# Chunk loop of a delta-rule recurrence: the inverse's levels in four array quarters and in transposed form

## The chip, the cores and the metric

The kernel runs on one core of one Trainium2 chip. The metric is the device time of one execution in microseconds, the median over several; less is better. The core has a matrix engine (TensorE, PE in the profile), three elementwise engines (VectorE is DVE, ScalarE is ACT, GpSimd is POOL) and SyncE (SP), which here only issues DMAs. PE reads SBUF and writes PSUM; DVE and ACT move PSUM to SBUF; POOL works on SBUF alone.

## The reference, cut to what matters

One layer: an input projection, a gated MLP branch, an RWKV-7 branch, their merge, and a mixture of 32 experts. The change is in the RWKV-7 branch over 512 prompt tokens, 16 heads of 64:

```python
def step(s, inp):
    r_t, w_t, k_t, v_t, a_t, b_t = inp
    sa = jnp.einsum('bhij,bhj->bhi', s, a_t)
    s = s * w_t[:, :, None, :] + sa[..., :, None] * b_t[..., None, :] + v_t[..., :, None] * k_t[..., None, :]
    y = jnp.einsum('bhij,bhj->bhi', s, r_t)
    return s, y
```

The kernel doesn't step token by token. It takes 8 chunks of 64 tokens. Within a chunk the tokens depend on each other through a strictly triangular 64x64 matrix per head; with ones on the diagonal it is N, and the chunk needs the inverse of N applied to a right-hand side. The state is then carried to the next chunk.

## The kernel before, in words

`phase_chunks` is one phase between two all-engine barriers. The projections, decays and normalised keys of all tokens lie in SBUF when it starts; the next phase (`phase_gating`) begins after it.

**Tiling.** 16 heads are 8 pairs, and the two heads of a pair lie on partitions 0-63 (`lo`) and 64-127 (`hi`). The pairs are in two groups g of four (`G`, `GP`). A 64x64 block product of a head uses one quarter of the 128x128 array: its input partitions choose the quarter's rows, its output partitions the quarter's columns. Each group has four PSUM banks, `bank[g][0..3]`; bank[0][0] and bank[0][1] are halves of `m.psv`, and the profile calls them psv and the others ck_b. One float32 product is two records of the trace on PE and two on PEld. A block of eight products (one group, both heads of four pairs) is 16 records.

**The inverse.** It is built in doubling blocks: X starts as N's inverse for blocks of 2 (mask `m.levels[:, 0]`), and five levels (`LEVELS`, blocks of 2, 4, 8, 16, 32 being joined, NL = 5) make it that of 64. Z is the transposed of X, a1 the transposed of N. A level, in `level(c, lv)`:

1. PE, for g 0 then 1: W = N X by `own_blocks` (L602), weights a1, moving X, into bank 1. Eight products each.
2. DVE, per group: W into SBUF, multiplied by the level's mask (L874).
3. PE, per group: X = Z^T W (weights Z, moving W, bank 2), and but for the last level Z = W^T Z (weights W, moving Z, bank 3). Sixteen products each.
4. ACT, per group: X (L804), then Z (L807) into SBUF.

`own_blocks` reads and writes the same partitions of a head, so it uses two of the four quarters: lo to lo, hi to hi. `scores` is a block that uses all four (L639 own, L641 crossed), with 128 columns moved; `turn_bk_v` moves v to the other half (L668).

**A chunk.** PE's order is: `turn_n` (L650) for both groups, which turns N into bank 0; `turn_bk_v` for both; level 0; level 1; `old_state` (L697 to L702); levels 2, 3, 4; `scores` of the next chunk for g 0; `corrected`, which applies X to the right-hand side; `scores` for g 1; `new_state` (L715 to L722).

Around it, each engine's order is written out by hand, one queue each, with semaphores:

- DVE: the first Z is a1 times a mask (L867, two); then W per level; after W of level 2 both row products of the next chunk on the lower half (L615, L616 in `a_r_rows`); after the levels the masked scores (L828, L834), copies of the corrected values (L838), the new state (L844, L846), y (L851).
- ACT: a1 out of bank 0 (L789, two); the state (L794); per group the turned b and k (L798) and v (L799, L800); X and Z of the levels; after level 0 the exponentials of the next chunk (L770, L772); after level 1 the right-hand side (L813, L814).
- POOL: the scaled b and k of the next chunk (L623, L624), its own half of the row products, then for each group N with its diagonal (`nb`, L901) and the first X (L906).

`scores(c + 1, 0)` waits for all four row products and all four b, k products.

Of the kernel before, what the change touches and what calls it, by code (L numbers as in the profile page):

```python
# [12 lines left out]
P = 128  # L13
D = 1024
NK = D // P
TP = 512
# [100 lines left out]
def constants(eng, m, step, s_ident, wide, wide1t):  # L117
# [8 lines left out]
    step.did(eng.memset(wide1t[:, :], 0.0))  # L126
# [19 lines left out]
    for n, b in enumerate((1,) + LEVELS):  # L146
        odd = wide[:, n, :].rearrange("p (a two b) -> p a two b", two=2, b=b)[:, :, 1, :]
        step.wait()
        step.did(eng.memset(odd, 1.0))
        select(odd, ALU.is_ge, 0, [[-2 * b, P // (2 * b)], [0, b]], 1, 0.0)  # L150
        select(odd, ALU.is_ge, b - 1, [[2 * b, P // (2 * b)], [0, b]], -1, 0.0)
        select(wide[:, n, :], ALU.not_equal, 0, [[-1, P]], 1, 1.0)
    even = wide1t[:, :].rearrange("p (a two) -> p a two", two=2)[:, :, 0]
    select(even, ALU.not_equal, -1, [[-2, P // 2]], 1, 1.0)
    select(wide1t[:, :], ALU.not_equal, 0, [[-1, P]], 1, 1.0)
    step.wait()
    for half in range(2):
        own = slice(HD * half, HD * (half + 1))
        step.did(eng.tensor_copy(m.levels[own, :, :], wide[own, :, own]))
        step.did(eng.tensor_copy(m.level1t[own, :], wide1t[own, own]))  # L160
        step.did(eng.tensor_copy(m.ident2[own, :], m.ident[own, own]))
# [3 lines left out]
def phase_tokens(nc, m, a):  # L165

    ctx, sb, ps, sem = open_phase(nc)
    with ctx:
# [8 lines left out]
        wide1t = sb("wide_level1t", [P, P])  # L177
# [10 lines left out]
        @block.gpsimd  # L188
        def _(eng):
            constants(eng, m, Steps(eng, s_const), s_ident, wide, wide1t)  # L190
# [358 lines left out]
def phase_chunks(nc, m, a):  # L549

    ctx, sb, ps, sem = open_phase(nc)
    with ctx:
# [7 lines left out]
        a1 = sb("ck_a1", [P, NP, CH])  # L560
        X = sb("ck_X", [P, NP, CH])
        Z = sb("ck_Z", [P, NP, CH])
        W = sb("ck_W", [P, NP, CH])
# [10 lines left out]
        def pair_sems(name):  # L574
            return [sem(f"k_{name}{g}") for g in range(G)]

        s_eo, s_tb, s_nt, s_w, s_xz, s_rhs, s_u, s_y, s_s = \
            (pair_sems(n) for n in ("eo", "tb", "nt", "w", "xz", "rhs", "u", "y", "s"))
        s_mb, s_lk, s_nb, s_tb_e, s_a1, s_x1, s_z1, s_w_e, s_xz_e, s_rh_e, s_u_e, s_y_e, s_st, s_s0 = \
            (pair_sems(n) for n in ("mb", "lk", "nb", "tb_e", "a1", "x1", "z1", "w_e", "xz_e", "rh_e", "u_e", "y_e",  # L580
                                    "st", "s0"))
        NL = len(LEVELS)
        NX = 2 * NL - 1
# [13 lines left out]
        def own_blocks(eng, out, weights, moving, g):  # L597

            for n in range(GP):
                p = g * GP + n  # L600
                for rows in (lo, hi):
                    last = eng.matmul(out[rows, n, :], weights[rows, p, :], moving[rows, p, :], start=True, stop=True)  # L602
            return last
# [8 lines left out]
        def a_r_rows(eng, c, rows, which):  # L612

            at = tokens(c)
            eng.tensor_tensor(L[rows, :, which, 0:CH], m.kk[rows, :, at], running(c, 0, CH)[rows], ALU.mult).then_inc(s_ar, 1)  # L615
            eng.tensor_tensor(L[rows, :, which, CH:P], m.r[rows, :, at], running(c, 1, CH + 1)[rows], ALU.mult)\  # L616
# [10 lines left out]
        def _(eng):  # L627
# [17 lines left out]
            def turn_n(c, g):  # L645
                eng.wait_ge(s_nb[g], c + 1)
                eng.wait_ge(s_mb[g], c + 1)
                for n in range(GP):
                    for rows in (lo, hi):
                        last = eng.matmul(b64(bank[g][0])[rows, n, :], nb[rows, g * GP + n, :], m.ident[rows, rows],  # L650
                                          start=True, stop=True)
                last.then_inc(s_nt[g], 1)

            def turn_bk_v(c, g):
# [10 lines left out]
                for n in range(GP):  # L665
                    p = g * GP + n
                    for rows, others in ((lo, hi), (hi, lo)):
                        last = eng.matmul(b64(b[3])[others, n, :], m.v[rows, p, tokens(c)], m.ident[rows, rows],  # L668
                                          start=True, stop=True)
                last.then_inc(s_tb[g], 1)  # L670

            def level(c, lv):
                for g in range(G):
                    if lv == 0:
                        eng.wait_ge(s_a1[g], c + 1)
                        eng.wait_ge(s_x1[g], c + 1)
                        eng.wait_ge(s_lk[g], 2 * c + 2)
                    else:
                        eng.wait_ge(s_xz_e[g], c * NX + 2 * lv - 1)
                    own_blocks(eng, b64(bank[g][1]), a1, X, g).then_inc(s_w[g], 1)  # L680
                for g in range(G):
                    if lv == 0:
                        eng.wait_ge(s_z1[g], c + 1)
                        eng.wait_ge(s_tb_e[g], c * 3 + 3)
                    else:
                        eng.wait_ge(s_xz_e[g], c * NX + 2 * lv)
                    eng.wait_ge(s_w_e[g], c * NL + lv + 1)
                    own_blocks(eng, b64(bank[g][2]), Z, W, g).then_inc(s_xz[g], 1)
                    if lv < NL - 1:
                        own_blocks(eng, b64(bank[g][3]), W, Z, g).then_inc(s_xz[g], 1)  # L690

            def old_state(c, g):
                b = bank[g]
                eng.wait_ge(s_s0[g], c * 2 + 2)
                for n in range(GP):
                    p = g * GP + n
                    eng.matmul(b64(b[0])[lo, n, :], L[:, p, 0, 0:CH], wv[:, p, 0, :], start=True, stop=True)  # L697
                    eng.matmul(b64(b[0])[hi, n, :], L[:, p, 1, 0:CH], wv[:, p, 1, :], start=True, stop=True)
# [6 lines left out]
            def corrected(c, g):  # L705
                eng.wait_ge(s_rh_e[g], c * 2 + 2)
                eng.wait_ge(s_xz_e[g], c * NX + NX)
                own_blocks(eng, b64(bank[g][2]), X, rh, g).then_inc(s_u[g], 1)
# [1634 lines left out]
```

## Time and profile before

| | us |
|---|---|
| median of 3 runs | 1246.95 (1246.49 to 1248.7) |
| profiled execution, its own time | 1246.74 |
| its span | 1244.7 |
| PE busy in the span | 1123.8 (90%) |
| chunk phase, about | 279 to 490 of the span |
| mean granted clock of PE | 0.961 of full speed |

In the profile a row of a timeline is the start in the span, its duration, the engine, the line, the operation, output<-inputs, the shapes and the number of merged instructions. What stands in brackets is how long the engine stood idle before it and what released it. The end of a matmul is modelled, so starts are compared here, and a merged row's duration reaches to the modelled end of its last record. PEclk is the granted clock as a share of 2.4 GHz.

### The profile page before, as it was taken

The numbers are of one execution on the slowest core, as the hardware profiler recorded it, in microseconds if no ns is written. First come the engines' busy times: TensorE is split into PE (matmuls) and PEld (weight loads), VectorE is DVE, ScalarE is ACT, GpSimd is POOL, SyncE is SP. The second block draws the span as 40 slices with busy tenths as digits, with TensorE's granted clock in tenths as the row PEclk, the third lists the DMA queues.
The fourth block names the chain that finished last, engine by engine and source line by source line (L and its number), as shares of the span: only waits on it lengthen the run. The fifth ranks groups of instructions, "written<-read, shape, count | busy, mean of one in ns | idle before, by whom it ended". The sixth has DMA issues, their size and how long they took to land. (4 is left out here: it accounts for less than half of the span.)

```text
span 1244.7 us, 25175 instructions
## 1 busy us (share of the span) xinstructions
PE 1123.8 (90%) x10677; PEld 872.2 (70%) x10677; DVE 488.4 (39%) x1145; ACT 297.5 (24%) x584; POOL 196.7 (16%) x215
## 2 busy tenths in 40 slices
PE   3599999969999999899989999999898799988874
PEld 3488888848888988788877788888455455544441
DVE  3135455455555563455536611100236422211126
ACT  2022223334555544100024501000011111111112
POOL 4000000014354340000000007500000222211110
PEclk9799999989999999999999999999997799998897
DMA  3322122120000000322921222360776799999985
GB/s 107 95 76 59 53 53 79 26 61 14 4 4 4 4 4 3 97 66 67 236 75 34 68 68 68 87 184 1 293 318 260 268 414 415 414 417 417 415 346 206
DMA packets 113838, 182.98 MB, mean 147 GB/s; under 512 B 10364, under 2 KB 88520, under 8 KB 105029
## 3 DMA queue, kind: packets, MB, share of 16 engines
q1 hardware_dynamic: 107190, 168.56, 38.7%
q0 software_dynamic: 5168, 8.56, 1.9%
q10 hardware_dynamic: 1383, 4.42, 0.9%
q8 instruction: 79, 1.29, 0.4%
q14 instruction: 18, 0.15, 0.0%
HBM read 173.24 MB, written 17.55 MB: 153 GB/s over the span
## 5 line engine op out<-in xcount | busy, mean ns | idle before, releaser
L271 PE MATMUL rk_ps<-xT,rk_w 128*128 128x260 f32 x768 | 175.5, 387 | 9.9 <-DMA rk_lw<-in_a_lora_up 9.9
L271 PEld LDWEIGHTS rk_ps<-xT,rk_w 128*128 128x128 f32 x768 | 145.6, 191 | 37.2 <-issue 9.9
L271 PE MATMUL mg_psg<-xT,w_merge 128*128 128x260 f32 x512 | 116.6, 387 | 2.7 <-PEq L110 2.7
L271 PEld LDWEIGHTS mg_psg<-xT,w_merge 128*128 128x128 f32 x512 | 98.3, 192 | 18.1 <-issue 2.7
L2083 DVE SCALAR_TENSOR_TENSOR ex_sg<-tl_psA,ex_slot_rs,ex_sg 128x128 f32<-128x128 f32 x32 | 11.2, 351 | 139.1 <-ACT ex_sg L1883 138.9
L271 PE MATMUL uv_psu<-xT,w_uv 128*128 128x260 f32 x256 | 59.2, 391 | 3.0 <-ACTq L1037 3.0
L602 PE MATMUL ck_b<-ck_W,ck_Z 64*64 64x64 f32 x1280 | 52.3, 220 | 9.0 <-DVE ck_W L874 6.3
L271 PE MATMUL mg_psp<-ya,w_merge 128*128 128x260 f32 x256 | 57.6, 383 | 0.0
L271 PE MATMUL psv<-xT,w_uv 128*128 128x260 f32 x256 | 57.5, 383 | 0.0
L271 PE MATMUL mg_psp<-r_all,w_merge 128*128 128x260 f32 x256 | 57.4, 382 | 0.0
L271 PEld LDWEIGHTS uv_psu<-xT,w_uv 128*128 128x128 f32 x256 | 49.1, 194 | 11.0 <-ACTq L1037 3.3
L602 PEld LDWEIGHTS ck_b<-ck_W,ck_Z 64*64 64x64 f32 x1280 | 45.3, 134 | 13.3 <-issue 13.3
L1355 POOL TENSOR_TENSOR S<-S,sv 128x4096 f32<-128x4096 f32 x1 | 8.9, 8866 | 285.7 <-DVE r_all L1324 285.7
L271 PEld LDWEIGHTS mg_psp<-r_all,w_merge 128*128 128x128 f32 x256 | 48.6, 190 | 7.5
L271 PEld LDWEIGHTS psv<-xT,w_uv 128*128 128x128 f32 x256 | 48.5, 190 | 7.4
L271 PEld LDWEIGHTS mg_psp<-ya,w_merge 128*128 128x128 f32 x256 | 48.5, 190 | 7.4
L1575 POOL DMA_INDIRECT d_y<-tl_xn,ex_sidx x32 | 31.9, 998 | 118.8 <-DVE tl_xn L2087 118.8
L259 DVE TENSOR_TENSOR rk_diff<-rk_cols 128x512 f32<-128x512 f32 x24 | 16.6, 692 | 86.5 <-ACT rk_cols L451 86.5
L874 DVE TENSOR_TENSOR ck_W<-psv,levels 128x256 f32<-128x256 f32 x40 | 16.8, 419 | 77.1 <-PE psv L602 77.0
L451 ACT ACTIVATE rk_cols<-rk_ps 128x520 f32<-128x520 f32 x24 | 14.5, 606 | 128.3 <-PE rk_ps L271 128.3
L1330 DVE TENSOR_TENSOR mg_t<-mg_psp,mg_g 128x520 f32<-128x520 f32 x8 | 5.6, 699 | 99.2 <-PE mg_psp L271 99.2
L1883 ACT ACTIVATE ex_sg<-tl_psA,ex_slot_rs 128x128 f32<-128x128 f32 x32 | 11.8, 368 | 131.6 <-PE tl_psA L1741 131.6
(471 smaller groups left out, 2053.0 us busy)
## 6 DMA issues: line engine op xcount, KB each, us to landing
wd<-in_moe_w_down SPq DMA_DIRECT2D x15, 1024.0 KB
rk_w<-in_w_in SPq DMA_DIRECT2D x24, 512.0 KB, 5.2
tl_x<-in_moe_w_down SPq DMA_DIRECT2D x9, 1024.0 KB, 23.2
w_uv<-in_w_in SPq DMA_DIRECT2D x16, 512.0 KB, 5.2
w_merge<-in_w_in SPq DMA_DIRECT2D x16, 512.0 KB, 4.5
xT<-in_moe_w_gate SPq DMA_DIRECT2D x5, 1024.0 KB, 20.1
xT<-in_moe_w_up SPq DMA_DIRECT2D x5, 1024.0 KB, 23.0
bonus_all<-in_moe_w_gate SPq DMA_DIRECT2D x5, 1024.0 KB
```

The source lines that it names most:

```text
L259: step.did(eng.tensor_tensor(diff[:, 0:TP], cols[:, 0:TP], cols[:, 1:TP + 1], ALU.subtract))
L271: last = eng.matmul(out[:, h, 0:TH], weights[:, k, :], xT[:, k, h * TH:(h + 1) * TH], start=(k == 0), stop=(k == NK - 1))
L451: eng.activation(split(cols[j][:, 1:T + 1]), halves(psp[(3 * h + j) % 2]), ACT.Copy).then_inc(s_cols, 1)
L602: last = eng.matmul(out[rows, n, :], weights[rows, p, :], moving[rows, p, :], start=True, stop=True)
L874: eng.tensor_tensor(W[:, grp(g), :], b64(bank[g][1]), m.levels[:, lv + 1, :].unsqueeze(1).to_broadcast([P, GP, CH]), ALU.mult)\
L1330: eng.tensor_tensor(split(t[:, :]), halves(psp), split(g[:, :]), ALU.mult).then_inc(s_mg, 1)
L1355: step.did(eng.tensor_tensor(m.S[:, :, :], m.S[:, :, :], over_i(wd), ALU.mult))
L1575: eng.indirect_dma_start(out=m.d_y2, out_offset=bass.IndirectOffsetOnAxis(ap=rows, axis=0), in_=yo[:, x, :], in_offset=None, bounds_check= ...
L1883: eng.activation(sg[:, out, :], psg[out][:, 0:P], ACT.Silu, scale=scale).then_inc(s_sg, 1)
L2083: eng.scalar_tensor_tensor(out=sg[:, out, :], in0=psg[out][:, P:2 * P], scalar=scale, in1=sg[:, out, :], op0=ALU.mult, op1=ALU.mult).then_ ...
```

## The change

`a1` and its turning are gone: the level now computes V = N^T Z, with N itself (`nb`) as weights. The first Z is now the first X turned (`turn_x`) and copied out of bank 0 by ACT. After level 0, V and X lie on the other head's partitions, and a group's new Z (crossed quarters, bank 2) and new X (straight quarters, bank 3) alternate product by product. ACT copies both groups' Z first and then both groups' X. DVE no longer masks the first Z, and copies group 0's v instead of ACT. DVE's two row products for the next chunk are split between level 2 and level 3. `old_state` writes its two heads swapped. `constants` loses `level1t` and builds the masks for the transposed form. Left out below are renamed semaphores, the sample branch's use of V for W, and the buffers' declarations.

```diff
-    def turn_n(c, g):
-        eng.wait_ge(s_nb[g], c + 1)
+    def turn_x(c, g):
+        eng.wait_ge(s_x1[g], c + 1)
         eng.wait_ge(s_mb[g], c + 1)
-        for n in range(GP):
-            for rows in (lo, hi):
-                last = eng.matmul(b64(bank[g][0])[rows, n, :], nb[rows, g * GP + n, :], m.ident[rows, rows],
-                                  start=True, stop=True)
-        last.then_inc(s_nt[g], 1)
+        for n, p, own, other in heads(g):
+            last = eng.matmul(b64(bank[g][0])[own, n, :], X[own, p, :], m.ident[own, own], start=True, stop=True)
+        last.then_inc(s_zt[g], 1)
...
     def level(c, lv):
-        for g in range(G):
-            if lv == 0:
-                eng.wait_ge(s_a1[g], c + 1)
-                eng.wait_ge(s_x1[g], c + 1)
-                eng.wait_ge(s_lk[g], 2 * c + 2)
-            else:
-                eng.wait_ge(s_xz_e[g], c * NX + 2 * lv - 1)
-            own_blocks(eng, b64(bank[g][1]), a1, X, g).then_inc(s_w[g], 1)
+
         for g in range(G):
             if lv == 0:
                 eng.wait_ge(s_z1[g], c + 1)
-                eng.wait_ge(s_tb_e[g], c * 3 + 3)
+                eng.wait_ge(s_lk[g], 2 * c + 2)
             else:
-                eng.wait_ge(s_xz_e[g], c * NX + 2 * lv)
+                eng.wait_ge(s_z_e[g], c * (NL - 1) + lv)
+            for n, p, own, other in heads(g):
+                last = eng.matmul(b64(bank[g][1])[other if lv else own, n, :], nb[own, p, :], Z[own, p, :],
+                                  start=True, stop=True)
+            last.then_inc(s_w[g], 1)
+        for g in range(G):
+            if lv == 0:
+                eng.wait_ge(s_bkt[g], c + 1)
+                eng.wait_ge(s_v_e[g], c * 2 + 2)
+            else:
+                eng.wait_ge(s_x_e[g], c * NL + lv)
             eng.wait_ge(s_w_e[g], c * NL + lv + 1)
-            own_blocks(eng, b64(bank[g][2]), Z, W, g).then_inc(s_xz[g], 1)
+            for n, p, own, other in heads(g):
+                at = other if lv else own
+                if lv < NL - 1:
+                    new_z = eng.matmul(b64(bank[g][2])[own, n, :], X[at, p, :], V[at, p, :], start=True, stop=True)
+                new_x = eng.matmul(b64(bank[g][3])[other, n, :], V[at, p, :], X[at, p, :], start=True, stop=True)
             if lv < NL - 1:
-                own_blocks(eng, b64(bank[g][3]), W, Z, g).then_inc(s_xz[g], 1)
+                new_z.then_inc(s_z[g], 1)
+            new_x.then_inc(s_x[g], 1)
...
-            eng.matmul(b64(b[0])[lo, n, :], L[:, p, 0, 0:CH], wv[:, p, 0, :], start=True, stop=True)
-            eng.matmul(b64(b[0])[hi, n, :], L[:, p, 1, 0:CH], wv[:, p, 1, :], start=True, stop=True)
+            eng.matmul(b64(b[0])[hi, n, :], L[:, p, 0, 0:CH], wv[:, p, 0, :], start=True, stop=True)
+            eng.matmul(b64(b[0])[lo, n, :], L[:, p, 1, 0:CH], wv[:, p, 1, :], start=True, stop=True)
...
-        own_blocks(eng, b64(bank[g][2]), X, rh, g).then_inc(s_u[g], 1)
+        eng.wait_ge(s_x_e[g], c * NL + NL)
+        for n, p, own, other in heads(g):
+            last = eng.matmul(b64(bank[g][2])[own, n, :], X[other, p, :], rh[other, p, :], start=True, stop=True)
+        last.then_inc(s_u[g], 1)
...
-            eng.wait_ge(s_nt[g], c + 1)
-            eng.activation(a1[:, grp(g), :], b64(bank[g][0]), ACT.Copy).then_inc(s_a1[g], 1)
+            eng.wait_ge(s_zt[g], c + 1)
+            eng.activation(Z[:, grp(g), :], b64(bank[g][0]), ACT.Copy).then_inc(s_z1[g], 1)
...
-            eng.activation(bkt[:, grp(g), :], b4(b[2]), ACT.Copy).then_inc(s_tb_e[g], 1)
-            eng.activation(wv[hi, grp(g), 0, :], b64(b[3])[hi], ACT.Copy).then_inc(s_tb_e[g], 1)
-            eng.activation(wv[lo, grp(g), 1, :], b64(b[3])[lo], ACT.Copy).then_inc(s_tb_e[g], 1)
+            eng.activation(bkt[:, grp(g), :], b4(b[2]), ACT.Copy).then_inc(s_bkt[g], 1)
+            if g == 1:
+                eng.activation(wv[hi, grp(g), 0, :], b64(b[3])[hi], ACT.Copy).then_inc(s_v_e[g], 1)
+                eng.activation(wv[lo, grp(g), 1, :], b64(b[3])[lo], ACT.Copy).then_inc(s_v_e[g], 1)
         for lv in range(NL):
+            if lv < NL - 1:
+                for g in range(G):
+                    eng.wait_ge(s_z[g], c * (NL - 1) + lv + 1)
+                    eng.activation(Z[:, grp(g), :], b64(bank[g][2]), ACT.Copy).then_inc(s_z_e[g], 1)
             for g in range(G):
-                eng.wait_ge(s_xz[g], c * NX + 2 * lv + 1)
-                eng.activation(X[:, grp(g), :], b64(bank[g][2]), ACT.Copy).then_inc(s_xz_e[g], 1)
-                if lv < NL - 1:
-                    eng.wait_ge(s_xz[g], c * NX + 2 * lv + 2)
-                    eng.activation(Z[:, grp(g), :], b64(bank[g][3]), ACT.Copy).then_inc(s_xz_e[g], 1)
+                eng.wait_ge(s_x[g], c * NL + lv + 1)
+                eng.activation(X[:, grp(g), :], b64(bank[g][3]), ACT.Copy).then_inc(s_x_e[g], 1)
...
-        for g in range(G):
-            eng.wait_ge(s_a1[g], c + 1)
-            eng.tensor_tensor(Z[:, grp(g), :], a1[:, grp(g), :],
-                              m.level1t[:, :].unsqueeze(1).to_broadcast([P, GP, CH]), ALU.mult).then_inc(s_z1[g], 1)
+        eng.wait_ge(s_tb[0], c + 1)
+        eng.tensor_copy(wv[hi, grp(0), 0, :], b64(bank[0][3])[hi]).then_inc(s_v_e[0], 1)
+        eng.tensor_copy(wv[lo, grp(0), 1, :], b64(bank[0][3])[lo]).then_inc(s_v_e[0], 1)
         for lv in range(NL):
             if lv == 0 and c == 0:
                 eng.wait_ge(s_sv, 1)
             for g in range(G):
                 eng.wait_ge(s_w[g], c * NL + lv + 1)
-                eng.tensor_tensor(W[:, grp(g), :], b64(bank[g][1]),
+                eng.tensor_tensor(V[:, grp(g), :], b64(bank[g][1]),
                                   m.levels[:, lv + 1, :].unsqueeze(1).to_broadcast([P, GP, CH]), ALU.mult)\
                    .then_inc(s_w_e[g], 1)
             if lv == 2 and c + 1 < NC:
                 eng.wait_ge(s_px, c + 2)
                 eng.wait_ge(s_rhs[0], c + 1)
                 eng.wait_ge(s_rhs[1], c + 1)
-                a_r_rows(eng, c + 1, lo, 0)
+                a_rows(eng, c + 1, lo, 0)
+            if lv == 3 and c + 1 < NC:
+                r_rows(eng, c + 1, lo, 0)
...
-        a_r_rows(eng, c + 1, hi, 1)
+        a_rows(eng, c + 1, hi, 1)
+        r_rows(eng, c + 1, hi, 1)
```

The new row helpers are the two halves of `a_r_rows`; `heads(g)` yields, for each of four pairs, n, the pair's index, a head's own half and the other half.

## Rows read from the trace of the kernel before

**Rows 1.** The page's part 1: busy time, share of the span and instructions of each engine.

```profile
PE 1123.8 (90%) x10677; PEld 872.2 (70%) x10677; DVE 488.4 (39%) x1145; ACT 297.5 (24%) x584; POOL 196.7 (16%) x215
```

**Rows 2.** Windows: busy us and count per engine, granted clock, DMA share, GB/s.

```profile
279.00:490.00 211.00, 201.13 (x5977) 188.11 (x5978) 113.82 (x221) 111.72 (x285) 83.61 (x88) 0.99 0.03 7
...
860.00:880.00 20.00, 17.33 (x75) 14.00 (x75) 3.35 (x7) 0.60 (x1) 1.65 (x15) 1.00 0.04 5
...
1100.00:1200.00 100.00, 83.29 (x550) 47.64 (x548) 16.65 (x30) 11.33 (x30) 16.12 (x16) 0.91 1.01 413
```

**Rows 3.** Waits in 279 to 490: who waited for whom; us, times, longest.

```profile
PE ck_b L602 <- DVE ck_W L874: 6.3, 21, 0.6
```

**Rows 4.** Timeline of PE, starts of blocks in the chunk that begins at 413.56.

```profile
418.08 0.68 PE L602 MATMUL ck_b<-ck_W,ck_Z 64*64 64x64 f32 x16 [0.26 <-DVE ck_W L874]
...
419.97 0.66 PE L602 MATMUL psv<-ck_X,ck_a 64*64 64x64 f32 x16
...
421.24 0.68 PE L602 MATMUL ck_b<-ck_W,ck_Z 64*64 64x64 f32 x16
...
423.25 0.27 PE L697 MATMUL psv<-ck_wv,ck_L 128*64 128x64 f32 x1
...
425.27 0.68 PE L602 MATMUL psv<-ck_X,ck_a 64*64 64x64 f32 x16
...
428.45 0.66 PE L602 MATMUL psv<-ck_X,ck_a 64*64 64x64 f32 x16
...
431.93 0.66 PE L602 MATMUL psv<-ck_X,ck_a 64*64 64x64 f32 x16
```

**Rows 5.** Timeline of DVE, ACT in level 1 of that chunk.

```profile
420.67 0.42 DVE L874 TENSOR_TENSOR ck_W<-psv,levels 128x256 f32<-128x256 f32 x1 [2.38 <-PE psv L602]
...
421.14 0.64 ACT L772 ACTIVATE cum_all<-cum_all 128x520 f32<-128x520 f32 x1
421.96 0.39 ACT L804 ACTIVATE ck_X<-ck_b 128x256 f32<-128x256 f32 x1 [0.18 <-PE ck_b L602]
```

**Rows 6.** Timeline of PE, where two kinds of block meet in four quarters.

```profile
416.38 0.51 PE L668 MATMUL ck_b<-ident,v_all 64*64 64x64 f32 x10
416.67 0.27 PE L602 MATMUL psv<-ck_X,ck_a 64*64 64x64 f32 x2
...
416.78 0.22 PE L668 MATMUL ck_b<-ident,v_all 64*64 64x64 f32 x1
416.78 0.22 PE L602 MATMUL psv<-ck_X,ck_a 64*64 64x64 f32 x1
...
416.84 0.22 PE L668 MATMUL ck_b<-ident,v_all 64*64 64x64 f32 x1
...
417.19 0.28 PE L602 MATMUL ck_b<-ck_X,ck_a 64*64 64x64 f32 x4
```

**Rows 7.** Timeline of PE, first and last of scores' 16 merged rows (32 records).

```profile
408.12 0.33 PE L641 MATMUL psv<-ck_L,ck_bk 64*64 64x128 f32 x2
...
408.96 0.31 PE L639 MATMUL psv<-ck_L,ck_bk 64*64 64x128 f32 x2
```

**Rows 8.** Timelines from a chunk's start to level 0: PE, POOL, DVE, ACT.

```profile
414.02 0.63 PE L650 MATMUL ck_b<-ident,ck_nb 64*64 64x64 f32 x16
...
413.63 0.80 POOL L906 TENSOR_TENSOR ck_X<-ck_nb,levels 128x256 f32<-128x256 f32 x1
...
416.86 0.74 DVE L867 TENSOR_TENSOR ck_Z<-ck_a,level1t 128x256 f32<-128x256 f32 x2
...
418.22 0.38 ACT L800 ACTIVATE ck_wv<-ck_b 64x256 f32<-64x256 f32 x1
```

**Rows 9.** Timeline of POOL, the same first X of group 1 in chunk 0.

```profile
284.32 0.73 POOL L906 TENSOR_TENSOR ck_X<-ck_nb,levels 128x256 f32<-128x256 f32 x1
```

**Rows 10.** Timeline of POOL: the last product that the next scores wait for.

```profile
427.28 1.74 POOL L616 TENSOR_TENSOR ck_L<-r_all,cum_all 64x512 f32<-64x512 f32 x1
```

**Rows 11.** Line L616: durations in ns, shortest, median, longest.

```profile
L616 DVE TENSOR_TENSOR ck_L<-r_all,cum_all x9: 684/1739/1766, 275.9 to 453.9; 64x512 f32<-64x512 f32 x9
```

## What the change does to the time

> **What bounds the kernel now.** I read the page's busy shares first: PE works 90% of the span [rows 1]. Then the windows: in the chunk phase, 211 us, PE is busy 201 us at a granted clock of 0.99, and the DMAs are idle [rows 2]. So the phase is PE's, unless small waits hide in it. The view of waits shows how small: PE stood idle 6.3 us in 21 places for DVE's mask of W [rows 3]. The timeline of PE then shows what a level is. Level 1 of the chunk that I follow starts at 419.97 with two blocks of W and waits for the mask until 421.24. It then runs four blocks for X and Z up to 423.25: 3.28 us [rows 4]. A block of 16 records takes 0.47 us, a start every 29 ns, and it keeps two quarters of the array busy. Levels 2 and 3 take 3.18 us (425.27 to 428.45) and 3.48 us (to 431.93). Level 3 is longer because DVE does both row products between the masks of levels 2 and 3. The reader should see that a level has two parts: PE work of six blocks (6 x 0.47 = 2.82 us), and a chain mask, product, copy, product that is nearly as long. Halving the work uncovers the chain.
>
> **The chain, from rows.** From the start of a W block to DVE's mask 0.70 us (419.97 to 420.67). From the mask's start to PE's next block 0.57 (to 421.24), of which 0.42 is the mask. From that block's start to ACT's copy 0.72 (to 421.96) [rows 4, 5]. ACT's copy takes 0.39; that PE starts after it as late as after DVE, 0.15 later, is my estimate, since no row shows PE waiting for ACT: 0.54, say 0.55. Sum: 2.54 us per level.
>
> **Part 1: X and Z in four quarters.** The 32 records of a group's X and Z now go round four quarters. The trace has this form of block: scores. Its 32 records, with 128 columns each, start from 408.12 to 408.96, so 28 ns apart [rows 7]. That is the spacing of the 64-column records in two quarters, with twice the columns. Each quarter is therefore as fast with four busy as with two, and 64-column records should start some 14 ns apart. A second place bears this out with 64 columns: where the turning of v (crossed quarters) meets the first W (straight ones), records of both start together at 416.78 and go on to 416.84 [rows 6]. But the two blocks together, 416.38 to 417.19, took 0.81 us for 32 records, 25 ns each, because they overlap only at the seam. So the ends are 0.47 us for a group's X and Z (all overlapped) and 0.94 (not at all). I take 0.47, since the seam shows the full rate while it lasts and scores holds it for a whole block.
>
> PE's work in a level is then 4 x 0.47 = 1.88 us, under the chain's 2.54, and the chain decides. It holds for group 1 as well, 0.47 behind. ACT has four copies, 0.47 apart, 1.88 us a level; it does both Z first, so the X come late, but only the next X and Z product needs them, 1.27 us after the level's start. A level costs 2.54.
>
> **Part 2: the chunk's start.** `turn_n` needed `nb`, `turn_x` needs POOL's next product too. For group 1 that ends at 413.63 + 0.80 = 414.43, and the old turning started at 414.02 [rows 8]. With 0.05 for the release PE starts at 414.48, 0.46 later. Queued behind it are the turning of b, k and v and level 0; all move by 0.46. On DVE the two masks of Z go (0.74 us together) and two v copies come, of 64x256 and about as long: nothing, and they run while PE still turns. DVE held the first mask of W until its masks of Z ended at 417.60 [rows 8]; now PE holds it, at 417.13 + 0.70, say 417.90 with the seam. X and Z of group 0 start at 418.47 (before 418.08 [rows 4]). Group 1's wait for ACT's v copies, which ended at 418.22 + 0.38 = 418.60. ACT has lost group 0's two copies but starts 0.46 later, so I put the end at 418.93 and PE at 419.05, 0.11 after it could have gone.
>
> **Level by level, this chunk.** Level 0: Z of group 0 is copied from 418.47 + 0.72 = 419.19, and level 1 starts at 419.19 + 0.55 = 419.74, against 419.97. Level 1: the mask at 420.44, X and Z of group 0 at 421.01, of group 1 at 421.59 (behind its own chain from 419.05), and `old_state` at 422.06 against 423.25: 1.19 us gained. ACT does the exponentials here, 0.66 and 0.64 us ([rows 5] has the second), which now stand before the copies of Z of level 1: about 0.7 us late. `old_state` hides it, for it takes 2.02 us on PE (423.25 to 425.27) and needs none of these copies. Without that cover it would cost 0.7 a chunk. Level 2: 3.18 to 2.54, 0.64 gained. Level 3: 3.48 to 2.54, 0.94 gained. Level 4 has no Z and two quarters as before; but DVE's second row product now lies before its mask. The gap between masks is 2.54 - 0.47 - 0.42 = 1.65 us, and the product takes 1.74 (0.68 at the shortest [rows 11]): 0.1 lost. Sum: 1.19 + 0.64 + 0.94 - 0.10 = 2.67 us.
>
> What is late next: scores of the next chunk, waiting for POOL's products. POOL's last one ended at 427.28 + 1.74 = 429.02 [rows 10], 5 us before scores, which came 2.15 us after level 4 began at 431.93. Now POOL ends some 0.7 later (behind the exponentials) and scores come 2.7 earlier: 1.6 us of slack stay. I take nothing.
>
> **The sum.** 8 x 2.67 = 21.4 us. In chunk 0 the first X of group 1 ends at 284.32 + 0.73 = 285.05 [rows 9] and its turning started at 284.29, so 0.81 is lost there and not 0.46: -0.35. The last chunk has no row products, so its level 3 had no stall to lose: -0.2. Of chunks whose level 3 stalled less than this one's I allow 0.1 in all. That leaves 20.7 us. The masks' setup on POOL loses four instructions at the kernel's start, where POOL runs far ahead: 0. The swapped halves of `old_state` and `corrected` are the same instructions: 0.
>
> Nothing downstream can take the gain back as far as the trace shows: an all-engine barrier ends the phase, what follows is PE-bound, and at 860 to 880 the DMAs are still at 5 GB/s [rows 2], so the expert stage's full-rate stream has not begun and moves with the rest. The profiled execution took 1246.74 us, 0.21 under the median of the runs; 1246.74 - 20.7 = 1226.0, and as a median **1226 us**.
>
> **A rule that speaks against it.** The four-quarter rows give starts of 0 to 10 ns apart in different quarters [rows 6]. The Trainium skill, TensorE: Matmul & The Clock Gate, section "Wait — 56ns, not 53.3ns?", says that matmuls never start less than about 25 ns apart, however small. By that rule a group's X and Z would take 32 x 25 ns = 0.80 us, which is the first rival. The trace disagrees at the seam, so it gets a small chance.
>
> **Rivals.**
> *The overlap is half.* A group's X and Z take 0.81 us, as the two blocks with a seam did [rows 6]. Group 0's Z is copied 0.81 + 0.25 after the block's start, and a level costs 1.27 + 0.81 + 0.25 + 0.55 = 2.88 us. Level 0 loses 0.11, level 1 takes 1.27 + 2 x 0.81 = 2.89 up to `old_state` and gains 0.39, levels 2 and 3 gain 0.30 and 0.60: 1.18 a chunk, 9.4 less 0.65: 1238. For: nothing shows 64 columns at the full rate over a whole block. Against: scores.
> *The quarters don't overlap at 64 columns.* X and Z take 0.94, levels 1 and 2 cost what they did, level 0 loses 0.38 with the late turning, level 3 gains its stall of 0.30: +0.6 and +0.6 for chunk 0 and the last, 1248. Against: the seam.
> *The clock falls* (the slower side). PE now idles twice a level, about 0.3 us each. Had its clock of 0.99 fallen, PE's own work in a chunk, about 19.6 us in my count (levels 9.4, the rest 10.2), takes twice as long while it is at 1.2 GHz. A share of 0.13 at the lower level eats 2.6 us, so it decides from a mean clock of about 0.93. At the 0.91 of the window 1100 to 1200 [rows 2] it would be 0.18 x 19.6 = 3.5 us a chunk: 8 x 3.5 = 28, so 1254. For: in that window PE waits. Against: it is busy 83% there, with far longer waits; 860 to 880 has PE busy 87% at 1.00, and the phase itself has idle places of up to 0.6 us at 0.99 [rows 2, 3].
>
> **How the numbers follow.** Forecast 0.80; half overlap 0.08; no overlap 0.05; clock 0.04; 0.03 for a gain lost in a way that I don't see. The likeliest case alone spans 1222 to 1230: 0.1 us a level on the chain is 0.1 x 4 x 8 = 3.2 us. The range, 1222 to 1238, takes in the half overlap and leaves out some 0.13. A measurement of this kernel tells 0.2% (2.5 us) from no change. Faster: the forecast, the half overlap and a part of the rest, 0.91. Same: 0.05. Slower: the clock, 0.04.
>
> **What would show it.** Right: in the chunk phase, now 186 us, levels 2 and 3 start 2.54 us apart; a block of X and Z has 32 records within 0.5 us; PE waits twice a level, for DVE and for ACT; the second turning waits for POOL; level 1 to `old_state` 2.3 us; granted clock still 0.99. Wrong: blocks of 0.8 or 0.94 us; a level above 2.8; the second row product holding level 4's mask by more than 0.2; a wait for ACT at level 2 (the exponentials uncovered); scores waiting for POOL; or the phase shorter by 20 us and the kernel not.

## The result: half of the forecast gain

The changed kernel took 1238.09 us (median of 4 runs, 1234.83 to 1238.17), the kernel before 1247.83 beside it (1246.49 to 1249.2): ratio 0.9916, 95% interval 0.9895 to 0.9936. It is faster, by 9.7 us where 20.7 were forecast, and 1238.09 lies just outside the range of 1222 to 1238.

### The profile after

Part 1 and part 3 of the page of the kernel after (part 3: DMA queue, packets, MB, share). They answer to [rows 1]:

```profile
PE 1107.1 (90%) x10677; PEld 850.0 (69%) x10677; DVE 488.7 (40%) x1145; ACT 284.7 (23%) x568; POOL 195.6 (16%) x210
...
q8 instruction: 79, 1.29, 0.5%
```

PE has as many records as before and is busy 17 us less; the array does the same work in more quarters. The queue named instruction moved 1.29 MB in 79 packets, 16 KB each. I did not read that line before. It turns out to be the one that matters.

The windows of the kernel after (columns as in [rows 2]) over its chunk phase, from the first scores to the first product of the next phase, and for the stretch after it:

```profile
280.45:481.50 201.05, 185.71 (x5976) 166.29 (x5976) 114.01 (x221) 98.82 (x269) 83.60 (x88) 0.99 0.03 7
...
860.00:880.00 20.00, 15.91 (x53) 9.73 (x53) 1.95 (x5) 0.60 (x1) 1.65 (x15) 1.00 0.46 167
```

The phase takes 201.05 us; by the same marks it took 210.88 before (278.98 to 489.87). It saves 9.83. The profiled span fell by 8.7 (1244.7 to 1236.0): 9.83 less 1.47 by which the phase began later, plus 0.3 behind it. What begins late differs from one execution to the next whichever the kernel (279.04 and 280.30 in two variants of the kernel before), so it isn't the change. The clock stayed at 0.99, and the full-rate stream of weights moved forward with the rest: 860 to 880 now holds its head. So the whole shortfall lies inside the phase.

The tiles have other names now: L670 is the level's first product (W before; its mask is V), L683 and L684 are Z's and X's. PE's timeline in the chunk that [rows 4] follows: the first products of levels 3 and 4 and level 4's last block. Then DVE's masks of levels 2 to 4 and its second row product (columns: start, us, engine, line, operation, tiles, count):

```profile
421.91 0.68 PE L670 MATMUL psv<-ck_Z,ck_nb 64*64 64x64 f32 x16
...
424.38 0.68 PE L670 MATMUL psv<-ck_Z,ck_nb 64*64 64x64 f32 x16
...
425.68 0.92 PE L684 MATMUL ck_b<-ck_X,ck_V 64*64 64x64 f32 x24 [0.15 <-DVE ck_V L875]
427.29 0.45 PE L684 MATMUL ck_b<-ck_X,ck_V 64*64 64x64 f32 x8 [0.69 <-issue]
```

```profile
420.17 0.42 DVE L875 TENSOR_TENSOR ck_V<-psv,levels 128x256 f32<-128x256 f32 x1 [4.48 <-PE psv L670]
...
422.64 0.42 DVE L875 TENSOR_TENSOR ck_V<-psv,levels 128x256 f32<-128x256 f32 x1 [0.64 <-PE psv L670]
...
423.45 0.67 DVE L610 TENSOR_TENSOR ck_L<-r_all,cum_all 64x512 f32<-64x512 f32 x1
...
425.11 0.42 DVE L875 TENSOR_TENSOR ck_V<-psv,levels 128x256 f32<-128x256 f32 x1 [0.99 <-PE psv L670]
```

Two things are to be seen. The levels are as fast as forecast, or faster: 2.47 us from level to level. And in the last block PE stops for 0.69 us behind 24 of its 32 records, and its releaser is "issue": nothing that the profile shows was missing. DVE and ACT had long delivered.

PE's longest waits in 279 to 475 (line, waited for, us in total, times, longest), without the one at the phase's head:

```profile
PE ck_b L684 <- issue: 3.9, 6, 1.2
PE ck_b L683 <- DVE ck_V L875: 2.5, 16, 0.2
PE ck_b L643 <- POOL ck_X L909: 1.7, 4, 0.7
PE ck_b L633 <- issue: 1.5, 2, 1.0
PE psv L670 <- issue: 0.8, 2, 0.5
...
PE ck_b L699 <- issue: 0.7, 1, 0.7
```

The kernel before has no row of PE with "issue" in its phase. I went through every block of all eight chunks and counted the places where neither PE nor PEld starts a record for over 0.23 us, from start to start, though the program has nothing to wait for there (waits for DVE, ACT or POOL between blocks, and the gaps of 0.20 us between full-array turnings and v's, stand in every kernel and don't count): none before, **17 in the kernel after, 12.5 us in sum**, 0.28 to 1.38 each. 16 lie inside a block, of levels, scores, `old_state` or `new_state`; one lies between `corrected` and the scores of group 1, where the other chunks have no gap.

Here is the queue's traffic in 0.4 us just before such a stop. The 40 slices of the window show when the packet began (slice 27: 424.67), and 18.4% of 16 engines for 0.4 us is a packet that took 1.18 us:

```profile
GB/s 0 0 0 0 0 0 0 0 0 0 0 0 0 0 0 0 0 0 0 0 0 0 0 0 0 0 0 1638 0 0 0 0 0 0 0 0 0 0 0 0
...
q8 instruction: 1, 0.02, 18.4%
```

PE goes on at 427.29, 2.6 us after that packet began. All 17 stops end 2.15 to 2.9 us after a packet of this queue began. The phase has 47 packets before and 47 after, one in 254 records of PE and PEld or in 258 of all that TensorE ran, its sequencer's included (every 4.4 us before, every 4.2 after); 16 KB for 256 instructions would be 64 bytes each. My theory from here: PE runs out of instructions. A level is 192 of them (96 weight loads, 96 products, all groups). Before, it took 3.18 us, 16.6 ns an instruction; now 2.47, 12.9 ns.

One count ties the stops to the packets. Number all of TensorE's records in order of their start, its sequencer's too. Every one of the 17 stops stands behind a record whose number leaves 46 when divided by 256, record 46 of 256 for short (give or take one or two where starts coincide), and so does every stop of the kernels below. The phase has 47 such boundaries and 47 packets, in pairs. No boundary was crossed less than 2.15 us after its packet began, stop or not, in any kernel here, and but for the phase's first a packet began only when PE was at most 0.4 us from the boundary before it, or past it, here by up to 2.7 us. So each stretch of 256 has to last until its packet has begun and some 2.2 to 2.9 us more, or PE stops.

### The profile page after: what moved, and what is told of

Its sections match the earlier page's. It is cut to its first block and busy times, and to the rows that moved or that the text cites. A ratio compares the mean times of both kernels' runs of the same rounds, so it can differ in the third digit from the quotient of the medians.

```text
span 1236.0 us, 25152 instructions
## 1 busy us (share of the span) xinstructions
PE 1107.1 (90%) x10677; PEld 850.0 (69%) x10677; DVE 488.7 (40%) x1145; ACT 284.7 (23%) x568; POOL 195.6 (16%) x210
## 3 DMA queue, kind: packets, MB, share of 16 engines
q8 instruction: 79, 1.29, 0.5%
## 5 line engine op out<-in xcount | busy, mean ns | idle before, releaser
L684 PE MATMUL ck_b<-ck_X,ck_V 64*64 64x64 f32 x1280 | 51.6, 223 | 4.8 <-issue 3.9
L254 DVE TENSOR_TENSOR rk_diff<-rk_cols 128x512 f32<-128x512 f32 x24 | 16.6, 693 | 86.9 <-ACT rk_cols L446 86.9
L684 PEld LDWEIGHTS ck_b<-ck_X,ck_V 64*64 64x64 f32 x1280 | 43.7, 134 | 5.2 <-issue 4.9
L683 PE MATMUL ck_b<-ck_V,ck_X 64*64 64x64 f32 x1024 | 41.3, 222 | 4.0 <-DVE ck_V L875 2.5
L1574 POOL DMA_INDIRECT tl_xn<-d_tok,ex_gidx x17 | 17.8, 1050 | 157.9 <-DVEq L2079 86.5
```

Of the source, the lines that this page charges most:

```text
L254: step.did(eng.tensor_tensor(diff[:, 0:TP], cols[:, 0:TP], cols[:, 1:TP + 1], ALU.subtract))
L683: new_z = eng.matmul(b64(bank[g][2])[own, n, :], X[at, p, :], V[at, p, :], start=True, stop=True)
L684: new_x = eng.matmul(b64(bank[g][3])[other, n, :], V[at, p, :], X[at, p, :], start=True, stop=True)
L1574: eng.indirect_dma_start(out=xg[:, p % 2, :], out_offset=None, in_=m.d_tok, in_offset=bass.IndirectOffsetOnAxis(ap=gidx[:, p:p + 1], axis= ...
```

## Experiments

"Stops" are counted as above; in e_load_after a few fall where PE would wait anyway, which makes its sum uncertain by some 2 us. Clean is the phase less its stops. Levels, stops and phase are those of one profiled execution each, medians and ratios those of several.

| kernel | level 2 or 3, us | stops, us | phase, us | clean, us | median, us | ratio to before [95%] |
|---|---|---|---|---|---|---|
| before | 3.18 | 0 | 210.9 | 210.9 | 1247 | 1 |
| after | 2.47 | 17, 12.5 | 201.1 | 188.5 | 1238.1 | 0.9916 [0.9895, 0.9936] |
| a_apart | 2.48 | 9, 6.5 | 199.5 | 193.0 | 1237.0 | 0.9913 [0.9894, 0.9931] |
| b_turn_order | 2.47 | 18, 12.2 | 197.6 | 185.4 | 1236.8 | 0.9915 [0.9886, 0.9944] |
| c_shift128 | 2.47 | 14, 12.1 | 201.2 | 189.2 | 1240.2 | 0.9934 [0.9913, 0.9955] |
| d_fewer | 3.23 | 5, 4.7 | 218.0 | 213.3 | 1255.5 | 1.0061 [1.0045, 1.0077] |
| e_load_after | 2.47 | 29, 40.6 | 240.1 | 199.5 | 1278.8 | 1.0250 [1.0215, 1.0285] |
| f_load_before | 3.18 | 19, 29.3 | 245.7 | 216.4 | 1282.7 | 1.0278 [1.0256, 1.0299] |
| g_apart_order | 2.48 | 15, 8.1 | 200.1 | 192.0 | 1236.5 | 0.9910 [0.9890, 0.9930] |
| h_rows_only | 3.16 | 5, 1.7 | 209.9 | 208.2 | 1247.2 | 0.9997 [0.9983, 1.0012] |

### Z's and X's products one block behind the other (a_apart)

```
 for n, p, own, other in heads(g):
     at = other if lv else own
+    new_z = eng.matmul(b64(bank[g][2])[own, n, :], X[at, p, :], V[at, p, :], ...)
+new_z.then_inc(s_z[g], 1)
+for n, p, own, other in heads(g):
+    at = other if lv else own
-    new_z = ...
     new_x = eng.matmul(b64(bank[g][3])[other, n, :], V[at, p, :], X[at, p, :], ...)
```

> The changed kernel, but a group's sixteen Z records and then its sixteen X records instead of product by product, so that two quarters work at a time. Theory (fetch): the forecast was missed because PE ran out of instructions. Its instructions arrive in pieces of 16 KB, 256 at a time, and in the changed kernel 17 stalls inside blocks, 12 us in all, each end 2.2 to 2.9 us after a piece's fetch began. Here a group's X and Z should take 0.8 to 0.94 us (0.47 in the changed kernel), levels 2 and 3 about 2.8 to 3.1 us (2.47), and with the slower rate most stalls go (under 4 us): levels cost 8 x 4 x 0.35 to 0.6 = 11 to 19 us more, stalls give 8 to 12 back: 1238 to 1247 us. Rival (quarters): the stalls come from four quarters being busy at once (PSUM or SBUF conflicts); they vanish here too, so this run sizes the four-quarter blocks and doesn't tell the two apart.

Levels 2 and 3 stayed at 2.48 us, levels 0 and 1 took 2.74. PE's timeline of a level 0 in this kernel, with Z at L683 and X at L687:

```profile
411.34 0.51 PE L683 MATMUL ck_b<-ck_V,ck_X 64*64 64x64 f32 x10 [0.15 <-DVE ck_V L876]
411.64 0.27 PE L687 MATMUL ck_b<-ck_X,ck_V 64*64 64x64 f32 x2
411.65 0.28 PE L683 MATMUL ck_b<-ck_V,ck_X 64*64 64x64 f32 x3
411.74 0.22 PE L687 MATMUL ck_b<-ck_X,ck_V 64*64 64x64 f32 x1
411.75 0.22 PE L683 MATMUL ck_b<-ck_V,ck_X 64*64 64x64 f32 x1
```

After ten records of Z alone, X's records start between Z's last ones, though each stands behind all sixteen of them in the program. Blocks in different quarters run past each other; writing them product by product isn't what fills the array, and the expected 2.8 to 3.1 us a level was wrong. So was "under 4 us" of stops: they fell from 17 to 9 (6.5 us) while the median stayed, since the clean phase grew by 4.5 us.

### The second turning behind the first group's (b_turn_order)

```
-for g in range(G):
-    turn_x(c, g)
 for g in range(G):
+    turn_x(c, g)
     turn_bk_v(c, g)
```

ACT copies group 1's first Z behind group 0's bkt in the same manner.

> The changed kernel with PE's order turn X of group 0, b, k and v of group 0, turn X of group 1, b, k and v of group 1, and ACT's copies in that order. By the forecast's step on the late first X, 0.46 us a chunk (0.81 in chunk 0) is PE waiting for POOL: 4 us to gain at most; the changed kernel's trace shows 4.2 us of such waits in 9 places. If it is on the path: 1234 to 1236 us. If stalls for instructions take part of it back (fetch theory): 1235 to 1238. If ACT's in-order copies make the first Z of group 1 late: no gain.

The 4.2 us in 9 places of the expectation counts PE's and PEld's rows of the same wait; PEld's alone is 2.5 us in five. PE's wait for POOL at the second turning is gone, and the eight stretches from turning to level 0 fell from 27.8 to 24.5 us in sum. 3.1 us of clean phase are won; 18 stops of 12.2 us are as before. The median, 1236.8, can't be told from the 1238.1. The profiled execution, 1233.9, was 3 us under that median, so the phase in the table flatters this kernel.

### 128 instructions more ahead of the loop (c_shift128)

```
+for n in range(32):
+    rows = (lo, hi)[n % 2]
+    eng.matmul(bank[1][3][rows, 0:HD], m.ident[rows, rows], m.ident[rows, rows], start=True, stop=True)
```

> The changed kernel with 32 more 64x64 products (128 PE instructions, identity into a bank that is overwritten later) where PE is idle before the first scores; nothing else. Fetch theory: the boundaries of the 256-instruction pieces shift by 128 instructions against the code, so the stalls stand at other places of the chunks than in the changed kernel, and each still ends 2.2 to 2.9 us after a fetch began; their sum may come out at 6 to 18 us, the total within 6 us of the changed kernel's. Rival (quarters, semaphores, any cause that belongs to the code's place): the stalls stand at the same places of the same chunks, sum 12 us, total unchanged within 1 us.

Half a packet's worth of instructions moved the stops: 17 became 14, most at other places (in `old_state` at 295.7, in level products at 321.6 and 402.1, behind `corrected` at 456.4), and the last chunk, which had one of 1.38 us, had none and took 21.35 us instead of 23.3. Each ends 2.29 to 2.95 us after a packet began. All 14 stand behind record 46 of 256 again. So the stops follow the count of instructions, not a place in the program.

### W and V from full-array products (d_fewer)

```
-for n, p, own, other in heads(g):
-    last = eng.matmul(b64(bank[g][1])[other if lv else own, n, :], nb[own, p, :], Z[own, p, :], ...)
+for n in range(GP):     # levels 1 to 4; nx holds both heads' blocks, crossed, zeros elsewhere
+    p = g * GP + n
+    last = eng.matmul(b64(bank[g][1])[:, n, :], nx[:, p, :], Z[:, p, :], start=True, stop=True)
```

Left out: POOL's copies into `nx`, and level 0, which keeps its small products.

> The changed kernel with the first product of levels 1 to 4 as one 128x128 product a pair: N's two heads stand crossed in a block matrix with zeros between (four POOL copies of 64x256 a chunk), so that 16 of 32 instructions of each such block go: 256 of about 1440 PE instructions a chunk, with the same PE time (0.47 us a block). Fetch theory: stalls fall from 12 us to 2 to 6, total 6 to 10 us lower, 1228 to 1232; the level stays at 2.47 us, or up to 0.1 more where PE changes between full and quartered products. Rival (quarters): the four-quarter blocks are the same, so the stalls stay at 12 us and the total at 1238 to 1241.

Half the expectation held. Stops fell to 5 (4.7 us), none of them in a product of X and Z, which are in four quarters as before, so the four quarters alone don't cause them. But the level became 3.23 us and the kernel slower than before. PE's timeline of a level 2 in it:

```profile
354.99 1.10 PE L675 MATMUL psv<-ck_Z,ck_nx 128*128 128x64 f32 x8
355.93 1.06 PE L675 MATMUL ck_b<-ck_Z,ck_nx 128*128 128x64 f32 x8
```

Eight full-array records of 64 columns take 0.94 us to the next block, 0.117 each, where 16 records in two quarters take 0.47. Half the instructions cost twice the time.

### Copies inside DRAM during the loop (e_load_after, f_load_before)

In SyncE's stream, behind the loads of the phase:

```
+for n in range(LOADS):     # 16; each waits for the one before
+    if n > 0:
+        eng.wait_ge(s_load, 16 * n)
+    eng.dma_start(m.d_y2[(n % 2) * 1024:(n % 2) * 1024 + 1024, :]..., a["w_in"][0, 0:512, ...]...)
```

> The kernel after, with SP copying 2 MB pieces of w_in inside DRAM into a buffer that is unused at this time, sixteen one after the other, during the chunk loop; nothing of the loop waits for them. Supply theory (PE stops where a 16 KB piece of its instructions has not arrived): the pieces share the DMA engines with the copies, their packets take longer than the 0.9 to 1.5 us of now, and the stops grow from 17 and 12 us to well over 20 us in sum; phase over 208 us, the kernel over 1245 us. Rival (the stops are of PE's own making: order of the quarters, semaphores): phase 201 +- 1 us, stops 12 us, the kernel 1238 us plus only what the last copy delays. If the packets of the instruction queue are not slower than before, the run tells nothing.

> The same sixteen copies inside DRAM during the chunk loop of the kernel before, which has no stop of PE inside a block. Supply theory: packets two or three times as long bring stops here too, where 3 to 5 us now pass unnoticed; phase 212 to 225 us against 210.9. Rival (stops belong to the four quarters' blocks alone): no stop inside a block, phase 211 us.

With the count of records, this is the run that decides. The kernel before, whose levels never stopped, stops as soon as DMA traffic competes with its instruction packets. PE's waits of f_load_before in 279 to 425 (L605 is the product of [rows 3], then L602; L642 scores; L701 `old_state`), then the windows of the same kernel with the copies (to 425) and without:

```profile
PE ck_b L605 <- issue: 10.8, 8, 2.5
...
PE psv L605 <- issue: 5.4, 3, 2.0
PE ck_b L642 <- issue: 3.7, 1, 3.7
PE psv L701 <- issue: 1.9, 1, 1.9
```

```profile
345.00:425.00 80.00, 64.25 (x1690) 58.40 (x1681) 36.88 (x72) 31.51 (x81) 26.09 (x30) 0.94 0.69 236
425.00:465.00 40.00, 37.91 (x1151) 35.66 (x1153) 20.43 (x39) 22.79 (x58) 19.09 (x18) 1.00 0.02 5
```

And one block of it, `corrected`, in PE's timeline:

```profile
310.79 0.80 PE L605 MATMUL ck_b<-ck_rh,ck_X 64*64 64x64 f32 x21
314.14 0.79 PE L605 MATMUL ck_b<-ck_rh,ck_X 64*64 64x64 f32 x10 [2.55 <-issue]
```

PE ran 1690 products in 80 us with the copies (21 a us) and 1151 in 40 without (29 a us); the last stop is at 424.3. This block stopped at about 311.4; the packets of the queue began at 305.09 and at 311.87, and PE went on at 314.14, 2.3 us after the second. All its stops stand behind record 46 of 256. The phase, 245.7 us, is far over the 212 to 225 expected, and one detail of the cause was wrong: the packets took no longer (at most 1.2 us up to 420), they began late, up to 8.5 us after the one before, where the kernel before has 6.2 at most. Against the boundaries: up to 5.4 us after PE had crossed the one before, against 2.1. The clean phase grew too, by 5 us, with a clock of 0.94 beside the copies; I haven't divided that. In the kernel after the same copies raise the stops from 12.5 to 40.6 us.

### Both orders together (g_apart_order)

The edits of a_apart and b_turn_order in one kernel.

> Both of the changes made apart so far, together: Z's sixteen records ahead of X's sixteen, and the second turning of X behind the turning of bk and v of group 0. Theory (the level's length is the chain of two blocks and two copies, and what is left over is PE's supply of instructions): a_apart's phase of 199.5 us loses the 3 us at the chunk starts that b_turn_order lost: phase 196 to 197, the kernel 1233 to 1235 us, with 8 to 18 stops of PE inside blocks, 6 to 12 us. Rival (the supply paces the phase whatever the order: each microsecond saved elsewhere comes back as a stop): phase 199 to 201, 1236 to 1238 us, the stops' sum larger than a_apart's 6.5 us by what the chunk starts gain.

The phase, 200.1 us, is the rival's 199 to 201, not the theory's 196 to 197, but not for the rival's reason alone: stops rose from a_apart's 6.5 to 8.1 us, not by the 3.3 us that the chunk starts gained, but level 0 lost 1.9 (3.06 us instead of 2.75 where it waits for ACT's copies of v). The best median of all, 1236.5, and within 0.15% of its neighbours: no order of these blocks has beaten the change measurably.

### The split row products alone (h_rows_only)

```
-a_r_rows(eng, c + 1, lo, 0)
+a_rows(eng, c + 1, lo, 0)
+if lv == 3 and c + 1 < NC:
+    r_rows(eng, c + 1, lo, 0)
```

> The kernel before with one part of the change alone: VectorE's row products of the next chunk split, the first behind level 2's mask, the second behind level 3's. Theory: level 2 loses the wait for the second product, level 3 gets a short one; 0.25 us a chunk, seven chunks: 1246 us, ratio 0.9985 to 1.0. Rival (the wait is a large part of the change's gain of 9.8 us): 1242 us or less.

Level 3 fell from up to 3.64 us to 3.16 in most chunks (1.6 us over eight), the phase by 1.0, the median by nothing: ratio 0.9997. The gain of the change is that of the rest of it. This kernel has the levels of the kernel before, 16.5 ns an instruction, and yet five short stops, two of them inside a level's block: the line between a loop that stops and one that doesn't isn't sharp.

### How fast instructions come (i_stretch)

One run only, 1259.05 us. At the head of the chunk phase (left out: the semaphore `s_pre` that ends each stretch):

```
+for width, count in ((HD, 256), (P, 256)):
+    for n in range(count):
+        rows, others = ((lo, hi), (hi, lo))[n // 2 % 2]
+        out = (rows, others)[n % 2]
+        last = eng.matmul(bank[1][2 + n % 2][out, 0:width], m.ident[rows, rows], m.ident[rows, 0:width], ...)
```

> The kernel after with 512 products more at the head of the chunk phase, waiting for nothing: 256 of 64 columns, turning through the four quarters, and 256 of 128 columns in the same manner. Each product leaves four instructions (two weight loads, two records), so each stretch is 1024 instructions, four pieces of 16 KB. Supply theory: the first stretch would need 64 records in 0.94 us (32 in 0.47 us, as the level's block), 7.5 us in all, and outruns the supply: it takes 10 us or more, with a stop of 0.5 us or more at every piece, each ending 2.1 to 2.9 us after the packet's start; the second would need 28 ns a record as the scores do, 14.3 us, 3.6 us a piece, and has at most short stops. Rival (the stops belong to the levels' waits and copies, not to the number of instructions): both stretches run without a stop, 7.5 and 14.3 us.

PEld's timeline of both stretches (every product has two weight loads and two records, so 227 loads are 454 instructions):

```profile
273.80 5.46 PEld L730 LDWEIGHTS ck_b<-ident 64*64 64x64 f32 x227 [6.72 <-issue]
281.68 5.41 PEld L730 LDWEIGHTS ck_b<-ident 64*64 64x64 f32 x256 [2.41 <-issue]
288.59 0.55 PEld L730 LDWEIGHTS ck_b<-ident 64*64 64x64 f32 x29 [1.50 <-issue]
289.37 6.46 PEld L730 LDWEIGHTS ck_b<-ident 64*64 64x64 f32 x227 [0.23 <-PE ck_b L730]
296.32 3.51 PEld L730 LDWEIGHTS ck_b<-ident 64*64 64x64 f32 x128 [0.49 <-issue]
300.05 3.52 PEld L730 LDWEIGHTS ck_b<-ident 64*64 64x64 f32 x128 [0.21 <-issue]
304.06 0.85 PEld L730 LDWEIGHTS ck_b<-ident 64*64 64x64 f32 x29 [0.49 <-issue]
```

The narrow products need 10.6 ns an instruction while they run (5.41 us for 512) and lose 2.4 and 1.5 us in two stops, not one at every packet as expected; the wide ones need 13.7 (3.51 for 256) and lose 0.2 to 0.5 in each of three. With the stops both come to the same pace: 1024 instructions in 15.3 us (273.80 to 289.14) and in 15.5 (289.37 to 304.91), 15 ns each. Seven packets began between 279.08 and 301.69, 3.35 to 4.2 us apart. One caution: up to 282.5 the DMAs are 90% busy with the loads ahead of the phase, so the first stop, which ends at 281.67, isn't demand alone. The wide stretch has no such traffic beside it. By these two stretches PE outruns its supply below some 14 to 15 ns an instruction. A level at 16.6 doesn't (before), at 20.2 doesn't (d_fewer, 160 in 3.23 us), at 12.9 does.

## Why the prediction was half right

The mechanism was right, and the missing half is one term that the sum didn't have. The clean phase is 188.5 us: 22.4 less than before, against 20.7 forecast. 12.5 us of stops take the rest. (Clean is a lower bound: some stops hide in part behind a wait. One of 0.84 us lengthened its level by 0.66, one of 0.50 by 0.29. And the forecast's own sign "the chunk phase, now 186 us" doesn't follow from its sum: 211 less 20.7 is 190.)

- **Four quarters (right for a block, short from block to block).** The timeline of level 1 in an undisturbed chunk of the kernel after: its first product for group 0, X and Z of group 0, of group 1, and `old_state` (the first records of each):

```profile
365.32 0.68 PE L670 MATMUL psv<-ck_Z,ck_nb 64*64 64x64 f32 x16
...
366.62 0.24 PE L683 MATMUL ck_b<-ck_V,ck_X 64*64 64x64 f32 x1
...
367.26 0.24 PE L683 MATMUL ck_b<-ck_V,ck_X 64*64 64x64 f32 x1
...
367.89 0.27 PE L694 MATMUL psv<-ck_wv,ck_L 128*64 128x64 f32 x1
```

  A block's 32 records start within 0.48 us, as forecast (412.42 to 412.90 in another chunk). But the next block starts 0.64 after this one, 20 ns a record, the pace of i_stretch's long run (21 ns). A level has room for that. The first rival (0.81 us a block) falls. The Trainium skill states in TensorE: Matmul & The Clock Gate, section "Wait — 56ns, not 53.3ns?", that starts are never less than about 25 ns apart. The trace disagrees: 15 ns inside the block.
- **The chain (right, one part too long).** These are its steps through level 0 of the chunk that [rows 4] follows, whose W starts at 411.12: DVE's mask and PE's X and Z, then ACT's copy of Z, then PE's next W:

```profile
411.85 0.42 DVE L875 TENSOR_TENSOR ck_V<-psv,levels 128x256 f32<-128x256 f32 x1
...
412.42 0.24 PE L683 MATMUL ck_b<-ck_V,ck_X 64*64 64x64 f32 x1 [0.15 <-DVE ck_V L875]
```

```profile
413.16 0.39 ACT L805 ACTIVATE ck_Z<-ck_b 128x256 f32<-128x256 f32 x1 [0.20 <-PE ck_b L683]
```

```profile
413.60 0.68 PE L670 MATMUL psv<-ck_Z,ck_nb 64*64 64x64 f32 x16
```

  From W to the mask 0.73 (forecast 0.70), mask to X and Z 0.57 (0.57), to the copy 0.74 (0.72), copy to W 0.44 (estimated 0.55, with 0.15 behind its end where 0.05 was true): 2.48 for 2.54.
- **Level 1 to `old_state`.** Clean 2.57 (365.32 to 367.89 above: 1.30 + 0.64 + 0.63), forecast 2.32: two blocks of X and Z at 0.64 and not 0.58 and 0.47. That mis-sized term is 0.25 a chunk, 2 us in all.
- **Chunk's start (right in kind).** The second turning waits for POOL, 2.5 us in five places (PEld's row of the same wait; PE's is above), where I had 4.0 in eight. From the turning to level 1 eight chunks gained 4.3 us, more than my 1.5: 1.5 us is that smaller wait, and level 0 takes 2.47 to 2.55 us where I had 2.61 (417.13 to 419.74), 1 us over eight.
- **Level 4 and the row product.** Its mask was not held: the product took 0.67 us at 423.45, since POOL's own had ended at 423.15, and DVE then idled 0.99. Over all such products of DVE in both kernels, those with POOL idle take 0.67 to 0.69 us and those beside a POOL product up to 1.77; the forecast took 1.74, as long as beside POOL. The stretch to scores is 2.25 clean, 0.1 longer as forecast, not for the reason given.
- **ACT's exponentials, scores behind POOL, the clock (right).** No wait for ACT at level 2, none for POOL's rows at scores, 0.99.
- **What failed: "The chain decides".** That step took PE's blocks and the chain for all that can bound a level. When PE's work fell under the chain, PE needed its instructions at 12.9 ns instead of 16.6, and the supply of them ran short about twice a chunk. The range failed for the same reason: its upper end was set by half overlap, a rival that has nothing to do with it and gave 1238 by chance. The Trainium skill has the mechanism in Runtime: NRT & Kernel Launch, section "Instruction fetch mechanics": blocks of 16 KiB, 256 instructions, which agrees with the packets here. It also says that crossing a block is mostly hidden, since an engine issues slower than blocks are filled. That was true of the kernel before and costs 12.5 us in this one. The page gives PE's store as 128 KiB, eight such blocks. No such lead shows in this phase: each boundary waited for a packet that began about when PE crossed the one before or later, and in i_stretch PE stopped after 454 instructions and again after 512. A rival built on the section would have asked for instructions per us.

Shown: stops come with the instruction packets (every stop's end, and its place behind record 46 of 256), follow the count of instructions (c_shift128), appear in the kernel before when packets are late (f_load_before), need no wait and no level (i_stretch) and no fourth quarter (f_load_before has two). Open: why a packet begins up to 2.7 us after PE has crossed the boundary before it and sometimes at once, and so why a_apart has half of the stops. Open too: whether a loop with fewer instructions at the same chain would return the 12.5 us, as the one try (d_fewer) lengthened the chain.

## What to carry to other kernels

Count PE's instructions, weight loads included, against the time of each dense stretch, not of the whole phase (12124 in 201 us are 16.6 ns each and show nothing): this chip delivered them at about 15 ns each in a run of 1024, and a stretch that asks for more stops for 0.3 to 1.4 us at a time, in most cases, with "issue" as the releaser inside a block. Spreading small products over more quarters raises that demand without lowering the count, so expect the gain only down to this pace. And DMA traffic beside such a loop isn't free: it delays the packets (28 us of stops more here, 29 in the kernel before).

## What the hardware showed beside it

- Blocks in different quarters overtake each other by some six records (a_apart: X's first at 411.64 beside Z's eleventh).
- A full-array fp32 record of 64 columns costs 0.117 us to the next, against 15 ns inside a block over four quarters (20 from block to block) and 29 ns over two.
- In f_load_before the 16 copies of 2 MB kept the DMAs at 0.69 of their time; PE lost a quarter of its pace, though no engine in the loop waits for a DMA.
